# Projections and attention of a hybrid block as one program per engine

## What is computed

```python
h = rms_norm(x, norm1_gain[l])
proj = h @ w_in[l]                       # 1024 -> 1536 (q, k, v) + 1696 (recurrence)
sb = proj[..., :SB_COLS]
q = rms_norm(sb[..., :SB_WIDTH].reshape(B, S, SB_HEADS, HEAD_DIM), sb_q_gain[l])...
k = rms_norm(sb[..., SB_WIDTH:2 * SB_WIDTH].reshape(...), sb_k_gain[l])...
v = sb[..., 2 * SB_WIDTH:]...

def stick_breaking_attention(q, k, v):   # per block of 128 queries
    z = einsum('bhtd,bhsd->bhts', q[:, :, t0:end], k[:, :, :end]) * d ** -0.5
    log_keep = where(causal, log_sigmoid(-z), 0.0)
    after = sum of log_keep over the keys to the right of s
    weights = where(causal, exp(log_sigmoid(z) + after), 0.0)
    out = einsum('bhts,bhsd->bhtd', weights, v[:, :, :end])
```

## Time and profile before

| | us |
|---|---|
| three runs | 3133.19, 3138.0, 3141.32 |
| median | 3138.0 |
| profiled execution | 3133.6 |
| its span, first to last instruction | 3131.9 |
| TensorE busy | 2876.0 (92%) |
| VectorE busy | 1207.9 (39%) |
| ScalarE busy | 1001.6 (32%) |
| GpSimd busy | 651.6 (21%) |
| mean granted TensorE clock | 0.965 |

### The profile page before, as it was taken

How to read it: one execution, slowest core, us unless ns; L and a number is a source line. 1 busy time by engine, 2 the same in 40 slices (tenths; PEclk the granted TensorE clock), 3 DMA queues, 4 the chain that set the end, 5 groups by cost and what they waited for, 6 DMA issues and landing times. The chain is left out here.

```text
span 3131.9 us, 75649 instructions
## 1 busy us (share of the span) xinstructions
PE 2876.0 (92%) x29606; PEld 1682.2 (54%) x29607; DVE 1207.9 (39%) x2076; ACT 1001.6 (32%) x2002; POOL 651.6 (21%) x859
## 2 busy tenths in 40 slices
PE   8999899999799899688888869995999999999998
PEld 3444344443466566577777735554555555555554
DVE  2323211111587787567766613343111111111111
ACT  1111100000466566455545424441222222222221
POOL 0000010000110110556556400001222222222222
PEclk9999999999799899899999979997999999999999
DMA  3212211110420210111111045522777786766773
GB/s 118 67 50 67 60 41 60 60 60 29 119 65 8 66 38 8 29 39 43 41 41 39 17 164 201 188 107 95 266 266 269 261 288 228 240 228 227 268 240 85
DMA packets 173294, 374.89 MB, mean 120 GB/s; under 512 B 27985, under 2 KB 109393, under 8 KB 153970
## 3 DMA queue, kind: packets, MB, share of 16 engines
q10 hardware_dynamic: 31088, 182.46, 15.0%
q1 hardware_dynamic: 128866, 146.25, 14.2%
q0 software_dynamic: 13120, 43.00, 6.6%
HBM read 298.79 MB, written 72.88 MB: 119 GB/s over the span
## 5 line engine op out<-in xcount | busy, mean ns | idle before, releaser
L2052 PE MATMUL gu_ps<-wg_,xT 128*64 128x384 f32 (+1 forms) x2592 | 574.4, 380 | 1.9 <-issue 1.9
L2053 PE MATMUL gu_ps<-wu_,xT 128*64 128x384 f32 (+1 forms) x2592 | 574.4, 380 | 0.0
L2052 PEld LDWEIGHTS gu_ps<-wg_,xT 128*64 128x64 f32 x2592 | 324.0, 137 | 280.6 <-issue 280.2
L388 PE MATMUL p_ps<-h_all,w_ch 128*128 128x512 f32 (+1 forms) x896 | 387.6, 596 | 10.1 <-DMA w_ch<-in_w_in 10.1
L310 PE MATMUL qkv_ps<-w_sb,hT 128*128 128x512 f32 x768 | 336.6, 595 | 1.4 <-DVE hT L282 1.4
L2053 PEld LDWEIGHTS gu_ps<-wu_,xT 128*64 128x64 f32 x2592 | 324.1, 137 | 0.0
L2073 PE MATMUL y_ps<-wd_,hT 128*64 128x512 f32 x648 | 295.4, 599 | 0.0
L2072 PE MATMUL y_ps<-wd_,hT 128*64 128x512 f32 x648 | 295.4, 598 | 0.0
L388 PEld LDWEIGHTS p_ps<-h_all,w_ch 128*128 128x128 f32 (+1 forms) x896 | 166.0, 185 | 231.2 <-issue 231.2
L662 DVE TENSOR_TENSOR_SCAN prod<-keep,prod 128x512 f32<-128x512 f32 x192 | 236.4, 1274 | 55.2 <-ACT keep L608 54.5
L1664 PE MATMUL o_ps<-wo_sb,mixT_t 128*128 128x512 f32 x512 | 228.5, 600 | 19.8 <-DMA wo_sb<-in_w_out 19.8
(11 more groups left out here) (302 smaller groups left out, 4511.6 us busy)
## 6 DMA issues: line engine op xcount, KB each, us to landing
wg_<-in_w_exp_gate ACTq DMA_DIRECT2D x29, 2048.0 KB, 8.9
wu_<-in_w_exp_up ACTq DMA_DIRECT2D x29, 2048.0 KB, 14.2
wd_<-in_w_exp_down ACTq DMA_DIRECT2D x29, 2048.0 KB, 18.8
x_t<-in_x SPq DMA_DIRECT2D x32, 512.0 KB, 4.8
pT<-shifted SPq DMA_DIRECT2D x13, 1024.0 KB, 3.9
rkv<-pT SPq DMA_DIRECT2D x96, 128.0 KB, 2.5
mixT_t<-mixT SPq DMA_DIRECT2D x16, 512.0 KB, 4.1
out<-x_t SPq DMA_DIRECT2D x16, 512.0 KB, 2.7
```

Of the source, the lines that this page charges most:

```text
L388: last = pe.matmul(p_ps[0:width, s, g, :], w[:, s, k, 0:width], h_all[:, k, g * GT:(g + 1) * GT], start=(k == 0), stop=(k == KT - 1))
L2052: pe.matmul(gu_ps[half][LO, 0:wide], xT[:, k, :], wg[s][:, k, cols], start=(k == 0), stop=(k == KT - 1))
L2053: last = pe.matmul(gu_ps[half][HI, 0:wide], xT[:, k, :], wu[s][:, k, cols], start=(k == 0), stop=(k == KT - 1))
```

## The change

The three stages become one block. A class `Front` holds what they share: the tiles, the PSUM, the identity matrix and the semaphores that one stage waits for in another. Each stage returns one function per engine, and each engine calls its three one behind the other. Credit for all of them is given ahead, in three small blocks.

Tiles are laid over each other by hand. `h_all` keeps its place; its lower half later holds the second set of q, k, v, and its upper half `keep`, `prod` and `prodT`. The token stage's weights (`low`) give way to `shifted`, `diff` and `p_raw`, and its working tiles (`high`) to the first set of q, k, v. `v_diff` is made in place over `v_before`.

What was ordered by the ends of the blocks is now ordered by waits on single semaphores. The first chunk's channel weights and `mu` are fetched at the start of the program; the second chunk's weights follow when the last token matmul is done. The last `turn_qk` stands behind the first group of the first chunk. The first pair of heads is loaded as soon as q, k and v are stored, ahead of the channels; the second when the channel matmuls are done; a later one when the pair two before it is complete. The attention is written out over all four pairs, 160 steps, without a loop. POOL makes the first pair's differences ahead of the first mask, and those of pair p+1 at step 20 of pair p.

```diff
+    def load_pair(self, nc, sp, q, qT_dram, kT_dram, v_dram):
+        s, rows = q % 2, slice(q * P, (q + 1) * P)
+        sp.dma_start(self.q[s], qT_dram[rows, :]).then_inc(self.qk_loaded[s], 16)
+        sp.dma_start(self.k[s], kT_dram[rows, :]).then_inc(self.qk_loaded[s], 16)
+        ... (v, v_before and v_last in the same way)
 # tokens, SP: behind the three parts of w_sb
+        first_weights(sp)
         sp.wait_ge(consts, 2)
         sp.dma_start(v_dram[0:1, :], no_row[:, :]).then_inc(gains, 16)
...
-                sp.wait_ge(stored, CREDIT + NT * 48)
-                sp.wait_ge(gains, 16 * 4)
 # channels, SP
-                load(0, 0)
-                load(1, 1)
+        sp.wait_ge(front.projected, NT * 3)
+        load(sp, 1, 1)
+        sp.wait_ge(front.stored, CREDIT + NT * 48)
+        sp.wait_ge(front.gains, 16 * 4)
+        sp.wait_ge(front.h_kept, 2 + NT)
+        load_first_pair(sp)
 # channels, TensorE
             for g in range(NG):
-                pe.wait_ge(copied, c * NG + g + 1)
+                if isinstance(n, int) and n == 0:
+                    if s == 0 and g == 0:
+                        pe.wait_ge(front.h_kept, 2 + NT)
+                    if s == 0 and g == 1:
+                        last_turn(pe)
+                    if s == 0 and g == 2:
+                        pe.wait_ge(front.qkv_copied, CREDIT + NT * 3)
+                    if s == 1 and g == 0:
+                        pe.wait_ge(front.qkT_ready, CREDIT + NT * 2)
+                else:
+                    pe.wait_ge(copied, CREDIT + c * NG - 2 * NG + g + 1)
 # channels, VectorE
+        dve.wait_ge(front.projected, NT * 3)
         dve.memset(p_raw[:, 0:1], 0.0).then_inc(zeroed, 1)
 # attention, SP
+        sp.wait_ge(front.channels_done, NCH * NG)
+        front.load_pair(nc, sp, 1, qT_dram, kT_dram, v_dram)
+        for s in range(2):
+            sp.wait_ge(front.channels_stored[s], 16 * (NCH // 2) + 16)
+        for g in range(GROUPS):
+            sp.wait_ge(o_ready, CREDIT + g + 1)
+            ... (store)
+            if g % 4 == 3 and pair + 2 < PAIRS:
+                front.load_pair(nc, sp, pair + 2, qT_dram, kT_dram, v_dram)
+            if g == GROUPS - 5:
+                rec.fetch_first(nc, sp, *rec_inputs)
 # attention, TensorE
+            if n == 0:
+                pe.wait_ge(front.channels_copied, CREDIT + (NCH - 1) * NG)
-                with pe.Fori(0, ROUNDS) as j:
-                    scores(j, 0)
+        scores(0)
...
 # attention, GpSimd
-                with pool.Fori(0, ROUNDS) as j:
-                    for n in range(N):
-                        if steps[n][2] == 0:
-                            mask(j, n)
-                        if n % (N // 2) == 0:
-                            differences(j, steps[n][0])
+        differences(0)
+        for n in range(N):
+            if steps[n][2] == 0:
+                mask(n)
+            if n % EACH == EACH // 2 and n + EACH < N:
+                differences(n // EACH + 1)
 # the whole
+            @block.tensor
+            def _(pe):
+                a_pe(pe)
+                b_pe(pe, last_turn)
+                c_pe(pe)
+            ... (the other engines in the same way)
```

More of the change, by code:

```diff
@@ L88, in identity, with __init__ @@
                               pattern=[[-1, P]], channel_multiplier=1)
[L91 to L93 removed]
+class Front:
+    def __init__(self, nc, ctx, program):
         sb, pb, sem = makers(nc, ctx, program)
[L95 to L131, removed]
[L132 to L321 removed]
@@ L449, in __init__ @@
         self.steps = []
-        for pair in range(2):
+        for pair in range(PAIRS):
             for t in range(NT):
@@ L457, in __init__ @@
         self.N = len(self.steps)
-        self.units = 2 * NT
-        self.groups = 2 * NT // 4
+        self.each = self.N // PAIRS
+        self.groups = PAIRS * NT // 4
     def unit(self, n):
@@ L543, in _ @@
-                load(0, 0)
-                with sp.Fori(0, ROUNDS - 1) as j:
-                    one_round(j, last=False)
-                one_round(ROUNDS - 1, last=True)
-                for s in range(2):
-                    sp.wait_ge(stored[s], CREDIT + 16 * ROUNDS * NGR // 2)
+                a_sp(sp, first_weights)
+                b_sp(sp)
+                c_sp(sp)
+            @block.gpsimd
+            def _(pool):
+                a_pool(pool)
+                b_pool(pool)
+                c_pool(pool)
@@ L550, in _ @@
+            @block.scalar
+            def _(act):
+                a_act(act)
+                b_act(act)
+                c_act(act)
+            @block.vector
+            def _(dve):
+                a_dve(dve)
+                b_dve(dve)
+                c_dve(dve)
             @block.tensor
             def _(pe):
-                pe.wait_ge(consts, 1)
-                def scores(j, n):
-                    pair, t, c, start, w, _ = steps[n]
-                    if n % (N // 2) == 0:
-                        pe.wait_ge(qk_loaded[pair], j * 32 + 32)
-                    pe.wait_ge(kept, CREDIT + j * N + n - 1)
-                    for h in range(2):
-                        hs = slice(h * HD, (h + 1) * HD)
-                        done = pe.matmul(z_ps[n % 2][:, h, 0:w], q_sb[hs, pair, t * P:(t + 1) * P], k_sb[hs, pair, start:start + w],
-                                         start=True, stop=True)
-                    done.then_inc(z_done, 1)
```

885 lines of the change are left out of this document (464 added, 421 removed).

## The result

| | before | changed |
|---|---|---|
| median (us) | 3139.3 | 3088.6 |
| lowest and highest of four runs | 3133.2, 3141.3 | 3087.3, 3095.0 |
| ratio, 95% interval | | 0.985 [0.983, 0.986] |
| profiled execution | 3133.6 | 3095.0 |
| its span | 3131.9 | 3093.3 |

The median fell by 50.7 us, to 3088.6, and the forecast was 3087 (worked out from 3138.0, the median of the three runs known then). The unedited changed kernel was run twice more, beside other kernels: 3085.3 against 3132.7, and 3085.2 against 3133.5, so 47.4 and 48.4 less. The two profiled executions differ by only 38.6 us, though. That is not what the forecast says, and where the other 12 went is the first question.

The account below looks back on a forecast made before the run. The front was taken as bound by TensorE inside its stages and by hand-overs between them, only the latter winnable. Terms -1.0 + 17.8 + 23.9 + 10.4 = 51.1 us, from 3138.0 to 3087 us; range 3075 to 3101.

Parts of the forecast that it names:

- Start: Program start: two more credit blocks delay the first DMA, tile 2's later load is covered; -1.0 us.
- Tokens to channels: Token-to-channel hand-over: channel matmuls follow without a gap, clock stays whole, last turn stays on the path; +17.8 us.
- Channels to attention: Channel-to-attention hand-over: first pair and its differences ready early, DVE's last chunk comes last; +23.9 us, bounds 22.4 to 26.5.
- Loop and differences: Attention rounds: loop edge goes (+12.2), differences leave pair starts (+4.2) for mid-pair (-6.0); +10.4 us in all.
- (a): Attention: mid-pair differences stop TensorE for all 4.7 us, clock not won back at its start; 3096 us, chance 0.12.
- (b): Attention start: first pair's differences hold it nearly as before, only 4 of 23.9 us left; 3107 us, chance 0.04.
- (c): Attention: straight code of 160 steps is fetched too slowly, above all for TensorE; 3202 us, chance 0.02.
- (d): Attention steps: TensorE's gaps shrink once waits are constants, a tenth of 82 us counted; 3079 us, chance 0.09.

Follow-up runs that it names:

- the single block of that kernel: Changed kernel with its three small credit blocks at the start put together into one, same semaphores and credit: 3089.7 us, ratio 0.987.
- the kernel with the late fetch: Changed kernel with the first pair's load moved behind the last channel matmul, no barrier added: 3105.5 us, ratio 0.992.
- the combined kernel: Changed kernel with differences in four quarters, the last chunk's token shift in two parts and one credit block: 3076.7 us, ratio 0.982.

## Why the prediction was right

**Start.** The row moved as said, from 1.45 to 2.48, but the term was too small. In the two compared traces it is 1.64 instead of 1.0, and over all executions 1.9 (362.7 against 360.8): the first matmul comes 1.2 us later on average, and the rest is matmuls at the slow pace, which ends later too. The three small blocks account for 0.45 of the first DMA's 1.03; the rest of it is not explained by a run, since the single block of that kernel still credits all semaphores. Tile 2's load left at 29.1, not about 21: the working put some 5 us on the three new DMAs, and they took 16, as the 0.91 and 3.21 us of the two `mu` parts were no measure for the same loads behind the large transfers of the start, 7.49 and 4.41. ACT took the tile at 42.8, so 14 us of cover were left and the cost stayed 0.

**Tokens to channels.** 17.76 against 17.8, and each mark stood where it was put: first channel matmul without a gap, last turn 6.9 us later, clock at 1.00. Taking the cover off the turn costs 6.0 us, near the bound that the working named (12.2 of 17.8, so 5.6 less), but made up otherwise: a wait of 4.3 us instead of 2.9, and 1.7 us of clock instead of 2.7.

**Channels to attention.** 24.38 against 23.9. "DVE's last chunk comes last" held: the first scan came 5.40 us behind the last channel matmul, where the working has 5.4 (783.6 behind 778.2), and splitting the chunk gave 4.3 us. The size was right partly by luck. The clock did fall, during the second of two idle stretches, which the working left open between 0 and 2.4; without that fall the term would have been 26.2. In the three executions of the changed kernel it is 22.6 to 24.5. The bounds of 22.4 to 26.5 don't follow from the pieces that are named, which give 22.9 to 26.1. And POOL's three first masks took 5.18 us where they take 1.25 in the kernel with the late fetch (at 789.19, without the token shift beside them): 0.74, 2.52 and 2.00 us, the first two beside DVE's subtraction and mix of the last chunk, the third beside its first scans. The working had no such term; it cost the scans of step 2 a wait of 0.24 us.

**Loop and differences.** 11.03 against 10.4. What was there to win is measured now: three steps take 342.4 us in the kernel before and 326.7 with the differences in quarters (326.5 in the combined kernel), so 15.7 to 15.9, where the working had 12.2 + 4.2 = 16.4. The 0.25 us a pair that the loop cost inside the rounds were not in it. What mid-pair takes back was put at 2.0 and is 1.59, three times. That the old place costs less was right as well: 1.0 by the marks, 1.4 in the working. The 12.2 were taken whole and were won whole, but the reason given (drain, fetch, clock, differences ahead of masks) covers two things that the run with the rounds written out separates, 7.1 and 5.1.

The rule of the Trainium skill (GPSIMD Engine Reference, section Key points) that GpSimd contends with VectorE instructions that read two SBUF inputs agrees with these rows: 4.53 us of POOL's work stretched a 128x128 scan to 4.75. With the quarters a scan is 1.1 us longer beside an instruction of 1.27.

**Rivals.** (a), a stop of all 4.7 us in mid-pair, is out: it was 1.59, and the scans' lead over the turns took the rest; its second half came true, since the clock did fall at the start of attention. (b) is out: the first pair's differences stood ready. The late fetch, which brings its condition about, gives 3105.5, near its 3107. (c), code fetched too slowly, is out: the steps are equal and the whole attention is 11 us shorter. Runtime: NRT & Kernel Launch of the Trainium skill (section Instruction fetch mechanics) has straight code fetched ahead; by it (c) costs nothing, and the trace agrees, with three steps of 110.43 through code that runs once. (d), shorter gaps inside a step, is nearly nothing: 0.25 us a pair when the loop is gone, where the tenth of its effect that it counts would have been 2.0 a pair.

The forecast also said that it would be wrong if a stage behind attention changed its time. In the first profile one did, by 11.3 us. The total of that one execution alone would have spoken against the terms; only the repeats show that most of the 11.3 us is this stage's own variation.

## What to carry to other kernels

At each hand-over ask which engine comes last once the barrier and the fetch are gone. Here it was VectorE's tail of the old stage, and splitting that tail gave 4 us more, nearly half of it through the clock. Background work on GpSimd beside a chain of scans should come in pieces shorter than the lead that VectorE has over its reader: in quarters it cost nothing that the marks show, in one piece 1.0 to 1.6 us each time. And work out a change by stages between marks that both kernels have, and profile each kernel more than once: a stage whose code wasn't touched varied here by 9 us between three executions of the same kernel, and the point where the start's slow pace ends by 2 us.

## What the runs showed of the hardware

- POOL and VectorE held each other: a scan that began beside a running instruction of POOL ended only behind it. A scan of 0.39 us took 4.75 beside 4.53 us of POOL, and one of 0.96 took 2.01 beside 1.27. The other way round, masks of 0.41 and 0.53 us took 2.52 beside VectorE's mix of 2.34, and 2.00 beside four scans without a gap. POOL's differences themselves were hardly slowed: 4.53 us beside a scan, 4.49 with VectorE idle.
- TensorE's granted clock fell to 0.50 during the second of two idle stretches, of 1.51 and 2.77 us with 0.92 us of matmuls between them, at the start of attention; with the first stretch alone (the split chunk) it stayed at 1.00. From 768 on, in steps of 4 us, three executions of the changed kernel read 0.50, 1.00; 0.50, 0.85, 1.00; and 0.50, 0.50, 0.84; mask t=5 followed the first scores by 16.85, 17.00 and 18.75 us.
- At the start of the program TensorE's weight loads come 0.85 us apart instead of 0.43 for 2.7 to 6.1 us behind the first token matmul, as they do elsewhere at a granted 0.50. The windows print 1.00 there, but the first record of the clock in the trace comes only where this pace ends. Between executions of one kernel that point moved from 20.7 to 22.8 us.
- The same small `mu` load held SP's queue for 7.49 us behind the large transfers of the start and for 0.91 us between the stages; its second part took 4.41 and 3.21.
